# Retention queries and keys of two mixers: turned from the accumulator bank by quarters on the vector engine, instead of copied, exchanged by a product and turned

## The reference, cut to what matters

```
hcat = x @ w_in
(r_q, r_k, r_v, r_g, c_q, c_kv, k_r, m_q, m_k, m_v, m_o, m_i, m_f) = split(hcat)
rq = rope(to_heads(r_q, 4), pos);  rk = rope(to_heads(r_k, 4), pos)      # 4 heads of 64
ret = retention(rq, rk, to_heads(r_v, 4))
q_nope, q_rope = ... rms_norm(c_q) @ mla_w_uq ...;  q_rope = rope(q_rope, pos)
k_nope, v_mla = ... rms_norm(c_kv) @ mla_w_ukv ...;  k_rope = rope(k_r, pos)
att_out = mla_attention(q_nope, q_rope, k_nope, k_rope, v_mla)
hcell = mlstm(...)
merged @ w_out

rope: x1, x2 = halves of a head;  concatenate([x1*cos - x2*sin, x1*sin + x2*cos])
```

## Time and profile before

| | |
|---|---|
| median of the runs | 2372.38 us |
| the profiled execution's own time | 2372.06 us |
| its span | 2370.5 us |
| PE busy | 2310.9 us, 97% |
| DVE busy | 1885.0 us, 80% |
| ACT busy | 1404.4 us, 59% |
| the first mixer's `pair(0)` starts | 953.09 us |
| the second mixer's | 1289.51 us |

### The profile page before, as it was taken

One profiled execution on the slowest core, in us unless ns is written; L12 is line 12 of the kernel. 1 busy time (PEld: TensorE's weight loads), 2 busy tenths in 40 slices (PEclk: granted clock), 3 DMA queues, 4 the chain that ended last, 5 costly groups with the idle time before them and its releaser, 6 DMA issues.

```text
span 2370.5 us, 35057 instructions
## 1 busy us (share of the span) xinstructions
PE 2310.9 (97%) x13058; PEld 1990.5 (84%) x13058; DVE 1885.0 (80%) x2153; ACT 1404.4 (59%) x1395; POOL 68.8 (3%) x80
## 2 busy tenths in 40 slices
PE   9999999999999999989999989999999999999997
PEld 8977999897789998779988777888888888888886
DVE  5867898768779987774457778888889888888898
ACT  5465544455654436534336537777777777777774
POOL 0100000000000000000000010000000000000000
PEclk9999999999999999999999979999999999999999
DMA  6345555444465555268544349999999999999995
GB/s 257 140 160 177 210 182 189 161 166 142 143 216 197 191 181 214 89 221 264 188 177 160 133 172 399 374 388 372 388 373 388 372 389 371 390 372 389 373 390 218
DMA packets 93531, 609.18 MB, mean 257 GB/s; under 512 B 9696, under 2 KB 18032, under 8 KB 22640
## 3 DMA queue, kind: packets, MB, share of 16 engines
q1 hardware_dynamic: 88208, 585.74, 66.0%
q0 software_dynamic: 5216, 21.99, 2.4%
HBM read 592.48 MB, written 15.20 MB: 256 GB/s over the span
## 4 chain that ended last, share of the span: by engine, by line
PE 89%; DVE 5%; ACT 2%; DVEq 1%; issue 1%; DMA 1%; POOL 0%; ACTq 0%; POOLq 0%; SPq 0%
PE bank L326 27%; PE bank L328 27%; PE bank L327 27%; DVE w_lo L632 1%; DVEq L624 1%; PE bank L1932 1%; DMA raw<-in_weights_dram 1%; DVE probs L719 1%; PE bank L475 1%; PE bank L435 0%; PE bank L398 0%; PE bank L445 0%; ACT w_hi L528 0%; PE bank L378 0%; ACT probs L585 0%
## 5 line engine op out<-in xcount | busy, mean ns | idle before, releaser
L632 DVE TENSOR_TENSOR w_lo<-raw,w_hi 128x2048 fp32r<-128x2048 f32 x548 | 1240.5, 2288 | 255.9 <-ACT w_hi L528 233.2
L528 ACT CAST w_hi<-raw 128x2048 fp32r<-128x2048 f32 x548 | 1038.6, 1912 | 211.9 <-DMA raw<-in_weights_dram 203.9
L326 PE MATMUL bank<-w_hi,hT_hi 128*128 128x512 f32 (+3 forms) x1296 | 512.0, 395 | 8.4 <-DVEq L663 4.8
L328 PE MATMUL bank<-w_hi,hT_lo 128*128 128x512 f32 (+3 forms) x1296 | 501.9, 387 | 0.0
L327 PE MATMUL bank<-w_lo,hT_hi 128*128 128x512 f32 (+3 forms) x1296 | 501.0, 387 | 0.0
L326 PE MATMUL bank<-hT_hi,w_hi 128*128 128x256 f32 x1536 | 440.0, 286 | 4.2 <-DVE x_tok L1501 1.9
L327 PE MATMUL bank<-hT_lo,w_hi 128*128 128x256 f32 x1536 | 436.6, 284 | 0.0
L328 PE MATMUL bank<-hT_hi,w_lo 128*128 128x256 f32 x1536 | 436.6, 284 | 0.0
L326 PE MATMUL bank<-w_hi,oT_hi 128*128 128x512 f32 x940 | 370.6, 394 | 0.4
L327 PE MATMUL bank<-w_lo,oT_hi 128*128 128x512 f32 x940 | 366.4, 390 | 0.0
L328 PE MATMUL bank<-w_hi,oT_lo 128*128 128x512 f32 x940 | 366.3, 390 | 0.0
(11 more groups left out here) (307 smaller groups left out, 1572.6 us busy)
## 6 DMA issues: line engine op xcount, KB each, us to landing
raw<-in_weights_dram SPq DMA_DIRECT2D x548, 1024.0 KB, 4.9
token_rows<-all_cols SPq DMA_DIRECT2D x11, 512.0 KB, 8.8
arena<-in_norms_dram POOLq DMA_DIRECT2D x4, 1024.0 KB, 8.5
nat<-token_rows POOLq DMA_DIRECT2D x7, 512.0 KB, 8.0
unit_rows<-probs POOLq DMA_DIRECT2D x7, 512.0 KB, 7.0
arena<-in_b_gate_dram POOLq DMA_DIRECT2D x6, 512.0 KB, 4.0
unit_rows<-all_cols SPq DMA_DIRECT2D x5, 512.0 KB, 10.0
tables<-in_tables_b_dram POOLq DMA_DIRECT2D x1, 1216.0 KB, 5.6
```

Of the source, the lines that this page charges most:

```text
L326: mm(out, st[0], mv[0], start=start, stop=False, skip_group_check=True)
L328: return mm(out, st[1], mv[0], start=False, stop=stop, skip_group_check=True)
L528: self.isa.copy(m.w_hi[:, slot, :], m.raw[:, slot, :]).then_inc(m.hi_ready, 1)
L632: self.isa.tensor_tensor(m.w_lo[:, slot, :], m.raw[:, slot, :], m.w_hi[:, slot, :].bitcast(F32), ALU.subtract).then_inc(m.lo_ready, 1)
```

## The change

In each mixer the two ACT copies of RQ and RK go, with ACT's two waits for the products ahead of them, and the two PE products that exchange their halves. DVE reads banks 5 and 1 itself: one product by cos from the bank, four products of 32 partitions by sin that write to the partitions 32 away, and one subtraction. Bank 5 and bank 1 are counted free by the last of the four, where before ACT's copy did it. DVE waits for `w_used` itself. The other two tiles (KR and QR, with `rot32`) are turned as before. The places of the two turns in DVE's order are unchanged.

```diff
@@ TensorB.mixer
-        rot64, rot32 = m.tab(B_TABLES, "rot64"), m.tab(B_TABLES, "rot32")
+        rot32 = m.tab(B_TABLES, "rot32")
@@
         two_tiles(1)
-        self.rotate(b_tile(m, RQ, 2), 0, rot64, 2)
@@
         self.used(self.turned(outs, c, 768, cq, 2))
-        self.rotate(b_tile(m, RK, 2), 4, rot64, 2)
@@ ScalarB.mixer
         self.split(1)
-        self.eng.wait_ge(m.w_used, self.w.product_done())
-        self.copy_out(5, [(b_tile(m, RQ, 2), m.bank[5])], m.kq_copied)
         self.eng.wait_ge(m.cols_b_loaded, 16)
         self.high_turned((2, 3), m.oT_hi, par[:, QKV_NORM:QKV_NORM + 3], (8, 9, 10))
         self.split(1)
-        self.eng.wait_ge(m.w_used, self.w.product_done())
-        self.copy_out(1, [(b_tile(m, RK, 2), m.bank[1])], m.kq_copied)
@@ VectorB.mixer
         self.split(1)
-        self.roped(0, RQ, 2, cos64, sin64)
-        self.split(1)
-        self.roped(4, RK, 2, cos64, sin64)
+        first = RAW + DEPTH * A_LAYER + layer * (B_MIXER + 3 * FF_SUBS)
+        scratch = m.probs[:, :, :].rearrange("p a b -> p (a b)")
+        self.eng.wait_ge(m.w_used, first + 4)
+        self.turned_by_positions(5, RQ, 2, cos64, sin64, scratch)
+        self.split(1)
+        self.eng.wait_ge(m.w_used, first + 5)
+        self.turned_by_positions(1, RK, 2, cos64, sin64, scratch)
         self.split(2)
         self.roped(6, QR, 2, cos32, sin32)
```

## The result

The changed kernel takes 2383.31 us (median of 5 runs, 2382.03 to 2386.17) against 2372.38 before (2370.18 to 2372.93). The ratio is 1.005, its 95% interval 1.0039 to 1.0061. That is 10.9 us slower; forecast were 8.7. A later repetition, beside kernels of the experiments, gave 1.0046 (1.0033 to 1.0059). The profiled execution took 2382.73 us, its span is 2381.1.

What follows compares the result with a forecast made beforehand. PE was taken to bound the whole kernel, and the chain into `pair(0)` the changed stretch. 2 x (3.5 wait + 1.7 clock) - 1.7 given back = 8.7 us on 2372.06 gave 2380.8, so 2381; range 2376.5 to 2385.5.

Steps and rivals of the forecast that it cites:

- What bounds: Over the whole kernel PE, busy 97% of the span; at the mixers' start the ACT and DVE chain into `pair(0)`.
- The turning's price: DVE's new turning from a bank: 4.20 us instead of 2.08, the bank freed 3.49 us behind its start.
- The wait for bank 5: PE stands still 5.6 us ahead of chunk 5's product, until DVE's turning of RQ frees bank 5.
- The wait for bank 1: In chunk 6 PE waits 0.8 us for bank 1, unless the low clock swallows it.
- 3.5 us a mixer: `pair(0)` starts 3.5 us late in each mixer from the bank waits, before any clock term.
- ACT's idle time: ACT idle some 7 us ahead of its three copies behind chunk 5's product, instead of 3.07 ahead of RK's.
- The clock, on the product: Half clock in chunk 5's product behind the standstill: 1.7 us each mixer, bounds nothing to 4.3 us.
- Rivals 1 and 2: Behind bank 5's wait: clock falls in idle time, 2377.7 to 2379.4, chance 0.20; two half-clock stretches a mixer, 2384.5, chance 0.08.
- The clock, given back: First mixer loses its half-clock stretch behind `pair(0)`, as PE's gap ahead goes: 1.7 us off the sum.
- The gap ahead of `pair(0)`: PE's idle 1.34 us ahead of `pair(0)` goes in both mixers.
- The third: Rival: PE isn't held for bank 5, `pair(0)` about 0.3 us earlier a mixer; 2371.8 or 2373.5 us, chance 0.09.
- The fourth: Rival: the 3.5 us partly given back between `pair(0)` and the mixer's end; at half, 2377 us, chance 0.08.

## Why the prediction was right

- **What bounds.** Right. The mixers' start hangs on the chain into `pair(0)`, and what goes from PE and ACT buys nothing: with the banks relieved the time is level with before.
- **The turning's price.** Right to the digit: 3.49 us to the freeing of the bank (934.74 to 938.23), 4.20 in all.
- **The wait for bank 5.** Right: 5.6 us forecast, 5.43 and 5.42 measured, ended by L704. Shown as the cause by taking the banks away and by putting the wait alone into the kernel before.
- **The wait for bank 1.** Forecast at 0.8 us or swallowed by the low clock; it was swallowed. Its weight showed only with bank 5 relieved, at 6.16 us.
- **3.5 us a mixer.** Right: 3.7 in both with the clock held.
- **ACT's idle time.** Forecast 7, measured 9.66 and 9.29; the 7 left out the product's half-clock time, which I had in another term.
- **The clock, on the product.** Taken as 1.7 a mixer. From the product's start to ACT's copies are 6.53 and 6.18 us, against 4.30 + 0.20, so 2.0 and 1.7. The size is right, but by some luck. By the shares in stretches of 2 us, the low clock lasted 6.8 us in each mixer (936.0 to 942.8, 1277.3 to 1284.1), twice as long as behind `pair(0)` before; but 2.4 and 3.2 us of it lay in the standstill, where it costs nothing. Rivals 1 and 2 each had a part of this, and the parts offset each other.
- **The clock, given back.** This is the mis-sized term. I took 1.7 us off, because the first mixer would lose its half-clock stretch ahead of the scores. It did lose that one, but others came later: before, the clock was at 0.50 near 955 and 1004, after, near 995 and 1009, and the second part took 83.44 us instead of 83.35. So the refund was about nothing instead of 1.7. Without it the sum is 10.4; the two mixers cost 5.7 and 5.3 up to `pair(0)`, and the medians are 10.9 apart.
- **The gap ahead of `pair(0)`.** Forecast as gone; 1.10 us of it stayed. With the product slow, PE no longer waited for bank 1 and made up 0.8 us, while ACT's and DVE's chain did not.
- **Rivals.** The time alone doesn't tell the forecast from the second: 2383.31 is nearer to its 2384.5 than to 2381. What tells them apart is the product, which lost 2.0 and 1.7 us by the clock, not the second's 3.4 and not the first's nothing. The third (not slower) is excluded by the interval. The fourth (given back later) is contradicted by the table: +0.1 and +0.3 behind `pair(0)`.

The Trainium skill's page TensorE: Matmul & The Clock Gate, section Loop structure matters more than you think, counts a copy out of PSUM by DVE as harmless to the warm state. Here it was the other way: DVE's reading of the bank held the next product back, and the clock fell to 0.50 in both mixers. The page assumes that the next matmuls follow immediately.

## What to carry to other kernels

When work moves from one engine to another, ask which buffer the old engine used to release and where in the new engine's queue the release now stands; that place, not the work's length, set the loss. Look for the second late buffer behind the first, since a trace shows only the first. And count PE standstills twice, once for the wait and once for the clock, but expect no refund for a standstill that goes while another comes. To read such a loss from two traces, measure from the last row that both have in common, since half-clock stretches ahead of it differ from one execution to the next.

## What the runs showed of the hardware

- Extra DVE work that lengthened a PE gap by 0.5 us a mixer cost 4.8 us (2376.58 against 2371.78); with PE kept busy in that gap by products of zeros it cost nothing measurable (2370.16 against 2370.11).
- Products of zeros held the granted clock at 1.00 while PE waited (940 to 945), and by them alone the changed kernel got back 7.4 of its 10.9 us (2375.93 against 2383.31).
- After standstills of 5.43 and 5.42 us the granted clock was 0.50 on the product behind them, which in the first mixer ran at 0.21 us a step instead of 0.12. The low clock lasted 6.8 us in each mixer, 2.4 and 3.2 of them in the standstill itself, and cost the products 2.0 and 1.7 us.
- A product of 128x512 in f32 with two tensors took DVE 0.68 us with one of them in a bank and 0.69 from SBUF; four of 32x512 from a bank, each written 32 partitions away, took 2.79 us.
